# Stick-breaking attention of a three-block network on one Trainium2 core: rounded parts of queries and keys stored by the first product, two heads loaded early, another order on TensorE

## Chip, cores and metric

The kernel runs on one core of one Trainium2 chip, in one launch. The metric is the device time of that core in microseconds (us). The engines are TensorE (PE; its weight loads are listed as PEld), VectorE (DVE), ScalarE (ACT), GpSimd (POOL) and SyncE (SP), which here only issues transfers.

## What is computed

A network of three blocks on 1024 tokens of width 1024. The change lies in the first block, whose first mixer is stick-breaking attention with 8 heads of width 64:

```python
def first_block(x, mem, g_in, w_in, ...):
    h = _rmsnorm(x, g_in[l])
    proj = h @ w_in[l]                              # 1024 x 3584
    q_sb, k_sb, v_sb, u_c, b_c, c_c, q_mem, gate = jnp.split(proj, SPLIT_POINTS, axis=-1)
    y_sb = _stick_breaking_attention(q_sb, k_sb, v_sb)      # 8 heads
    m = _rmsnorm(mem, g_mem[l]); mk, mv = jnp.split(m @ w_mem_kv[l], 2, axis=-1)
    ...

def _stick_breaking_attention(q, k, v):   # per head, query t, key s < t
    # A[t,s] = sigmoid(z_ts) * prod_{s<j<t} (1 - sigmoid(z_tj)),  z = q.k / 8
    return A @ v
```

All of it is float32. Products that need the accuracy are made on TensorE in float32r from two rounded parts: hi is the value rounded to float32r, lo is the rest, value - hi.

## The kernel before, in words

`kernel` builds phases that follow each other. A phase (`Phase`) holds its own tiles and semaphores, and an instruction block with one program for each engine; the next phase begins on every engine when all have ended the last one. Within a phase each engine runs its program in order, and waits are written out by hand with counting semaphores.

The phases around the change, in order: `b1_turn`; `b1_in`, the first product (`late_norm_gemm_phase`); `mem_turn`, `mem_norm` (`norm_phase`) and `mem_kv`, which make the keys and values of the memory attention; `stick` (`stick_phase`); `conv`; `mem`. The products of `b1_in` go to the DRAM tensor `proj1`, transposed, 28 tiles of 128 rows by 1024 tokens. Rows 0 to 511 are the queries, 512 to 1023 the keys, 1024 to 1535 the values. For each tile (pair i, side s) TensorE does 48 products of 128x512 (`half_tile`), VectorE splits the tile's weights (`split`, L66 and L1075) and scales the sums into `out_sb` (`scale_out`, L1081), and ScalarE issues the store (`store`, L969). VectorE's loop is `split(i, s)`, then `scale_out(i - 1, s)`.

`norm_phase` can issue transfers for later phases on SP's queue (its list `ahead`), ahead of the loads of its gain vector (L369). `mem_kv` loads its weights by SP at L116 and splits them on VectorE (L66, L140) before TensorE begins.

`stick_phase` runs over 64 units. A unit j is one head and one block of 128 queries, `units[j] = (head, i)`, with n = i + 1 blocks of 128 keys. Heads go in four pairs, 16 units each, and the two heads of a pair alternate so that n runs 1, 8, 2, 7, 3, 6, 4, 5, 5, 4, 6, 3, 7, 2, 8, 1 in pairs 0 and 2, and 8, 1, 7, 2, ... in pairs 1 and 3. For each unit:

- `score(j)` on TensorE: q times k_hi and k_lo, and a mask, into one or two pieces of up to 512 columns (L1856, L1857, L1859), in a ring of four PSUM banks. `q_two` holds q_hi in its upper 64 partitions and q_lo in its lower 64, and `k_hi` and `k_lo` hold the head twice, so that the contraction over 128 partitions adds both.
- `sigmoids(j)` on ScalarE (L1922): "stay" = sigmoid(-z) of all pieces, then "take" = sigmoid(z), written over a part of `y`. Needs the scan of unit j-3 done.
- on VectorE the scan `later` (a running product of "stay", L1980), then weights = take * later (L1984).
- `turn` on TensorE (L1873): transposes the weights in groups of four blocks, into two PSUM buffers; `copy_turned` on ScalarE copies them to `wT` (L1936), which has three buffers. The values of a pair are turned likewise (L1931).
- `product(j)` on TensorE (L1883): weights times values, two instructions for each block; VectorE copies two results out after every fourth unit (L1958).

ScalarE's loop is `sigmoids(j + 2)`, `copy_turned` of unit j. TensorE's loop is:

```python
for j in range(NU):
    if j + 3 < NU:
        score(j + 3)
    while x < len(turns) and (turns[x][0] == "v" or turns[x][1] <= j):
        turn(x)
        x += 1
    if j >= 2:
        product(j - 2)
```

The rounded parts are made inside this phase. SP loads each head's keys and queries twice into halves of a spare tile (`b_gate` in the trace, L1803, L1805), four transfers of 256 KB. For heads 0 and 1 ScalarE rounds (L1908, L1910) and VectorE subtracts (L1962, L1964) before TensorE can begin. For heads 2 to 7 GpSimd does four instructions a head (L1829, L1831, L1833, L1835) while the units of the pair before run.

Of the kernel before, what the change touches and what calls it, by code (L numbers as in the profile page):

```python
# [8 lines left out]
F32 = mybir.dt.float32  # L9
# [5 lines left out]
P = 128  # L15
# [315 lines left out]
def norm_phase(nc, name, sum_matrix, src, dst, groups, g_vecs, tokens=T, scale_cols=None, shift_cols=None, src_dram=None,  # L331
# [12 lines left out]
    with Phase(nc, name) as ph:  # L344
# [15 lines left out]
        def _(sp):  # L360
# [503 lines left out]
def late_norm_gemm_phase(nc, name, ones, src, w_dram, n_cols, g_vec, out_dram, final_g=None, gate_pair=None, gate_shift=0):  # L864
# [11 lines left out]
    WAYS = 2 if double else 1  # L876
    with Phase(nc, name) as ph:
# [12 lines left out]
        out_sb, sig = ([ph.sb(f"{n}{s}", [P, T]) for s in range(2)] for n in ("out", "sig"))  # L890
        acc = [[ph.ps(f"acc{s}{h}", [P, HALF]) for h in range(NH)] for s in range(2)]
# [11 lines left out]
        gate_sig, gated_ready = [ph.sem(f"gate_sig{s}") for s in range(2)], [ph.sem(f"gated_ready{s}") for s in range(2)]  # L903
        w_view = w_dram.rearrange("(c p) n -> p c n", p=P)
# [32 lines left out]
        def _(act):  # L937
# [32 lines left out]

            def gate_and_store(i, s):
# [6 lines left out]
            for s in range(2):  # L978
                act.sem_inc(copied[s], NH)
                act.sem_inc(out_free[s], 16)  # L980
# [12 lines left out]
            if gate_pair > 0:  # L993
                with act.Fori(0, gate_pair) as i:
                    for s in range(2):
                        store(i, s)
# [6 lines left out]
            for s in range(2):  # L1003
                act.wait_ge(out_free[s], 16 * uses[s] + 16)

# [41 lines left out]
        def _(dve):  # L1047
# [34 lines left out]

            def gate_out(i, s):
# [29 lines left out]
            with dve.Fori(1, gate_pair + 1) as i:  # L1113
# [624 lines left out]
def stick_phase(nc, name, ident, neg_future, qT, kT, vT, y, spare, n_heads):  # L1738
# [11 lines left out]
    V_AT = (5, 9)  # L1750
    units = []
# [19 lines left out]
    with Phase(nc, name) as ph:  # L1771
        q_raw, k_raw = ([spare[:, 4 * n + 2 * b:4 * n + 2 * b + 2, :].rearrange("p a t -> p (a t)") for b in range(2)] for n in range(2))
        take = [y[:, NQ // 2 + b, :] for b in range(SIG)]
        q_two, k_hi, k_lo = ([ph.sb(f"{n}{b}", [P, T], F32R) for b in range(HEADS)] for n in ("q_two", "k_hi", "k_lo"))
        v_raw = [ph.sb(f"v_raw{b}", [P, T]) for b in range(2)]
# [9 lines left out]
        q_loaded, k_loaded, v_loaded = ([ph.sem(f"{n}_loaded{b}") for b in range(2)] for n in ("q", "k", "v"))  # L1785
        hi_ready, split_done, pool_split = ph.sem("hi_ready"), ph.sem("split_done"), ph.sem("pool_split")
# [8 lines left out]
        def _(sp):  # L1795
            def load(hd):
                b = hd % 2
                if hd in (2, 3):
                    sp.wait_ge(split_done, 2 * (hd - 1))
                elif hd >= 4:  # L1800
                    sp.wait_ge(pool_split, 4 * (hd - 3))
                for r in range(2):
                    sp.dma_start(k_raw[b][64 * r:64 * r + 64, :], kT[hd * 64:hd * 64 + 64, :]).then_inc(k_loaded[b], 16)  # L1803
                for r in range(2):
                    sp.dma_start(q_raw[b][64 * r:64 * r + 64, :], qT[hd * 64:hd * 64 + 64, :]).then_inc(q_loaded[b], 16)  # L1805

            def load_v(c):
                if c >= 2:
                    sp.wait_ge(turned_ready, turn_of["v", c - 2, 1] + 1)
# [11 lines left out]

        @block.gpsimd
        def _(pool):
            for hd in range(2, n_heads):
                b, r, done = hd % HEADS, hd % 2, 4 * (hd - 2)
                if hd >= HEADS:
                    pool.wait_ge(piece_ready, pieces_to[PER * (hd // 2 - 1)])
                pool.wait_ge(k_loaded[r], 32 * (hd // 2 + 1))
                nc.gpsimd.tensor_copy(k_hi[b][:, :], k_raw[r][:, :]).then_inc(pool_split, 1)  # L1829
                pool.wait_ge(pool_split, done + 1)  # L1830
                nc.gpsimd.tensor_tensor(k_lo[b][:, :], k_raw[r][:, :], k_hi[b][:, :].bitcast(F32), ALU.subtract).then_inc(pool_split, 1)  # L1831
                pool.wait_ge(q_loaded[r], 32 * (hd // 2 + 1))
                nc.gpsimd.tensor_copy(q_two[b][:, :], q_raw[r][:, :]).then_inc(pool_split, 1)  # L1833
                pool.wait_ge(pool_split, done + 3)
                nc.gpsimd.tensor_tensor(q_two[b][64:P, :], q_raw[r][64:P, :], q_two[b][64:P, :].bitcast(F32),  # L1835
                                        ALU.subtract).then_inc(pool_split, 1)
                pool.wait_ge(pool_split, done + 4)

        @block.tensor
        def _(pe):  # L1840
            def score(j):
                hd, i = units[j]
                b = hd % HEADS
                if j % PER < 2:
                    if hd < 2:
                        pe.wait_ge(split_done, 2 * hd + 2)
                    else:
                        pe.wait_ge(pool_split, 4 * (hd - 1))
# [13 lines left out]
            def turn(x):  # L1862
# [3 lines left out]
                if kind == "v":  # L1866
                    pe.wait_ge(v_loaded[a % 2], 16 * (a // 2 + 1))
# [25 lines left out]
            for j in range(NU):  # L1893
                if j + 3 < NU:
                    score(j + 3)
# [3 lines left out]
                if j >= 2:  # L1899
                    product(j - 2)  # L1900
            product(NU - 2)
# [3 lines left out]
        def _(act):  # L1905
            def split(hd):
                act.wait_ge(k_loaded[hd], 32)
                nc.scalar.activation(k_hi[hd][:, :], k_raw[hd][:, :], ACT.Copy).then_inc(hi_ready, 1)  # L1908
                act.wait_ge(q_loaded[hd], 32)
                nc.scalar.activation(q_two[hd][:, :], q_raw[hd][:, :], ACT.Copy).then_inc(hi_ready, 1)  # L1910

# [26 lines left out]
            split(0)  # L1938
            split(1)
# [13 lines left out]
        def _(dve):  # L1953
# [6 lines left out]
            def split(hd):  # L1960
                dve.wait_ge(hi_ready, 2 * hd + 1)
                nc.vector.tensor_tensor(k_lo[hd][:, :], k_raw[hd][:, :], k_hi[hd][:, :].bitcast(F32), ALU.subtract).then_inc(split_done, 1)  # L1962
                dve.wait_ge(hi_ready, 2 * hd + 2)
                nc.vector.tensor_tensor(q_two[hd][64:P, :], q_raw[hd][64:P, :], q_two[hd][64:P, :].bitcast(F32),  # L1964
                                        ALU.subtract).then_inc(split_done, 1)

# [6 lines left out]
            split(0)  # L1973
            split(1)
# [3477 lines left out]
def first_block(nc, A, C, M, xT):  # L5452
# [4 lines left out]
    mem_kv = scratch("mem_kv", 2 * MEM_W, N_MEM)  # L5457
    all_chunks = [(list(range(KD)), D)]
    first_turn_phase(nc, "b1_turn", ident, A["x"][0], xT)
    late_norm_gemm_phase(nc, "b1_in", ones, xT, A["w_in"][0], W1, A["g_in"][0], p, gate_pair=GATE1 // (2 * P))  # L5460
    with Phase(nc, "b1") as b1:
        y, gate = b1.sb("y", [P, KD, T]), b1.sb("gate", [P, KD, HALF])
        with Phase(nc, "b1m") as m:
# [204 lines left out]
```

## Time and profile before

| | us |
|---|---|
| median of 3 runs | 4560.4 |
| lowest, highest | 4555.65, 4563.99 |
| the profiled execution | 4569.06 |
| its span, first to last instruction | 4567.2 |
| TensorE busy in it | 3881.7 (85%) |
| VectorE busy | 2753.9 (60%) |
| ScalarE busy | 1915.0 (42%) |
| GpSimd busy | 482.3 (11%) |
| `mem_norm`'s first transfer to that of `stick_phase` | 359.56 to 397.18 |
| `stick_phase`, first transfer to last copy out | 397.18 to 604.6 |

The busy shares are means over many phases with different limits; the part that the change touches is the first 605 us. There the views to read are the busy time by stretch, the groups of instructions by line, and the timeline. In a row, "x16" counts instructions, "128x1024 f32<-128x1024 f32" is partitions by elements of output and input, and a time in brackets is how long the engine was idle before, with what released it. "b_y" is the tile into which "take" and the weights are written, "top_squares" holds the constants.

### The profile page before, as it was taken

The page shows a single profiled execution, that of the slowest core. Times are in us where ns is not written, and L with a number is a line of the kernel's source. Part 1 is how long each engine was busy: PE and PEld are TensorE (multiplying, and loading weights), DVE is VectorE, ACT ScalarE, POOL GpSimd, SP SyncE. Part 2 cuts the span into 40 slices and gives each one's busy share as a digit, 9 for nine tenths or more (in the row PEclk, how much of TensorE's full clock was granted, in tenths as well). Part 3 has the DMA queues.
Part 4 walks back from the last instruction along what each step waited for, and adds up shares of the span by engine and source line. Part 5 has one row for each costly group of instructions (what it writes and reads, how often), then busy time and mean ns, then how long its engine had stood idle before and what let it go on. Part 6 is the DMA issues. An engine that isn't in the chain of part 4 may idle for free. (4 is left out here: it accounts for less than half of the span.)

```text
span 4567.2 us, 51409 instructions
## 1 busy us (share of the span) xinstructions
PE 3881.7 (85%) x18727; PEld 3094.5 (68%) x18727; DVE 2753.9 (60%) x3208; ACT 1915.0 (42%) x2588; POOL 482.3 (11%) x347
## 2 busy tenths in 40 slices
PE   8995876899987897889849999999997998756479
PEld 6884744678854773767528888888885786635467
DVE  4235956431115775656469999999996334556852
ACT  2013634211114663224317777777774103454223
POOL 0001313140001212110000101100100400000020
PEclk9997988899998998989969999999997998878789
DMA  3224042122242106146239999999996233534241
GB/s 118 92 87 111 19 142 68 35 87 100 93 160 62 26 14 225 51 149 195 91 141 406 392 386 388 378 386 389 380 383 212 74 97 112 151 103 124 68 147 37
DMA packets 435455, 762.89 MB, mean 167 GB/s; under 512 B 101831, under 2 KB 264199, under 8 KB 434152
## 3 DMA queue, kind: packets, MB, share of 16 engines
q1 hardware_dynamic: 407480, 689.85, 42.9%
q10 hardware_dynamic: 23216, 54.27, 3.1%
q0 software_dynamic: 4608, 16.78, 1.4%
q8 instruction: 91, 1.49, 0.1%
q14 instruction: 60, 0.49, 0.0%
HBM read 643.64 MB, written 114.69 MB: 166 GB/s over the span
## 5 line engine op out<-in xcount | busy, mean ns | idle before, releaser
L71 PE MATMUL b_in_acc<-b_in_acts_hi,b_in_w_hi 128*128 128x512 f32 (+1 forms) x1456 | 573.6, 394 | 48.2 <-POOL b_in_w_lo L1132 20.9
L72 PE MATMUL b_in_acc<-b_in_acts_lo,b_in_w_hi 128*128 128x512 f32 (+1 forms) x1456 | 571.0, 392 | 0.0
L73 PE MATMUL b_in_acc<-b_in_acts_hi,b_in_w_lo 128*128 128x512 f32 (+1 forms) x1456 | 570.7, 392 | 0.0
L3965 DVE TENSOR_TENSOR experts_w_lo<-top_xT,experts_w_hi 128x2048 fp32r<-128x2048 f32 x192 | 437.3, 2290 | 62.4 <-ACT experts_w_hi L3910 62.4
L66 DVE CAST b_in_w_hi<-b_in_w 128x1024 fp32r<-128x1024 f32 (+1 forms) x91 | 65.2, 716 | 652.9 <-PE b_in_acc L73 641.6
L3965 DVE TENSOR_TENSOR experts_w_lo<-experts_ring,experts_w_hi 128x2048 fp32r<-128x2048 f32 x192 | 435.8, 2288 | 31.5 <-ACT experts_w_hi L3910 29.4
L3910 ACT ACTIVATE experts_w_hi<-top_xT 128x2048 fp32r<-128x2048 f32 x192 | 367.6, 1919 | 127.2 <-PE experts_gate L73 74.1
L3910 ACT ACTIVATE experts_w_hi<-experts_ring 128x2048 fp32r<-128x2048 f32 x192 | 367.8, 1921 | 114.7 <-PE experts_up L73 64.7
L71 PEld LDWEIGHTS b_in_acc<-b_in_acts_hi,b_in_w_hi 128*128 128x128 f32 (+1 forms) x1456 | 275.4, 189 | 111.7 <-POOL b_in_w_lo L1132 21.5
L72 PEld LDWEIGHTS b_in_acc<-b_in_acts_lo,b_in_w_hi 128*128 128x128 f32 (+1 forms) x1456 | 275.5, 189 | 58.7 <-issue 0.5
L73 PEld LDWEIGHTS b_in_acc<-b_in_acts_hi,b_in_w_lo 128*128 128x128 f32 (+1 forms) x1456 | 275.1, 189 | 58.8
L71 PE MATMUL experts_gate<-experts_w_hi,experts_xg_hi 128*128 128x512 f32 x512 | 201.8, 394 | 4.8 <-DVE experts_w_lo L3965 4.8
L71 PE MATMUL experts_y_ps<-experts_w_hi,experts_act_hi 128*128 128x512 f32 x512 | 205.3, 401 | 0.0
L71 PE MATMUL experts_up<-experts_w_hi,experts_xg_hi 128*128 128x512 f32 x512 | 200.8, 392 | 2.6 <-DVE experts_w_lo L3965 2.6
L73 PE MATMUL experts_y_ps<-experts_w_hi,experts_act_lo 128*128 128x512 f32 x512 | 200.3, 391 | 0.0
L73 PE MATMUL experts_gate<-experts_w_hi,experts_xg_lo 128*128 128x512 f32 x512 | 200.3, 391 | 0.0
L72 PE MATMUL experts_gate<-experts_w_lo,experts_xg_hi 128*128 128x512 f32 x512 | 200.0, 391 | 0.0
L72 PE MATMUL experts_y_ps<-experts_w_lo,experts_act_hi 128*128 128x512 f32 x512 | 199.6, 390 | 0.0
L73 PE MATMUL experts_up<-experts_w_hi,experts_xg_lo 128*128 128x512 f32 x512 | 199.4, 389 | 0.0
L72 PE MATMUL experts_up<-experts_w_lo,experts_xg_hi 128*128 128x512 f32 x512 | 199.4, 389 | 0.0
L760 ACT ACTIVATE b_in_out<-b_in_acc 128x512 f32<-128x512 f32 x76 | 45.5, 599 | 358.5 <-PE b_in_acc L73 357.8
L974 ACT ACT_TABLE_LOAD x8 | 10.3, 1283 | 375.6 <-DVE b_in_out L1081 366.0
(737 smaller groups left out, 8707.6 us busy)
## 6 DMA issues: line engine op xcount, KB each, us to landing
experts_ring<-in_w_gate SPq DMA_DIRECT2D x128, 1024.0 KB, 7.0
top_xT<-in_w_up SPq DMA_DIRECT2D x128, 1024.0 KB, 9.9
experts_ring<-in_w_down SPq DMA_DIRECT2D x64, 1024.0 KB, 9.3
top_xT<-in_w_down SPq DMA_DIRECT2D x64, 1024.0 KB, 9.2
b_in_w<-in_w_in SPq DMA_DIRECT2D x90, 512.0 KB, 3.9
proj<-b_in_out ACTq DMA_DIRECT2D x90, 512.0 KB, 2.7
b_gate<-proj SPq DMA_DIRECT2D x48, 256.0 KB, 5.0
x_spill<-top_xT SPq DMA_DIRECT2D x3, 4096.0 KB, 14.0
```

The source lines that it names most:

```text
L66: return nc.vector.tensor_copy(hi, x)
L71: nc.tensor.matmul(out, w_hi, x_hi, start=start, stop=False)
L72: nc.tensor.matmul(out, w_hi, x_lo, start=False, stop=False)
L73: return nc.tensor.matmul(out, w_lo, x_hi, start=False, stop=stop)
L760: nc.scalar.activation(out_sb[s][0:m, at(h)], acc[s][h][0:m, :], ACT.Copy).then_inc(copied[s], 1)
L974: nc.scalar.activation(sig[s][:, at(h)], out_sb[s][:, at(h)], ACT.Sigmoid).then_inc(gate_sig[s], 1)
L3910: nc.scalar.activation(w_hi[n % HIS][:, :, :], ring[n % RING], ACT.Copy).then_inc(hi_ready, 1)
L3965: nc.vector.tensor_tensor(w_lo[n % HIS][:, :, :], ring[n % RING], w_hi[n % HIS][:, :, :].bitcast(F32), ALU.subtract).then_inc(lo_ready, 1)
```

## The change

In the first product, `round_and_store` (ScalarE) and `part_out` (VectorE) take the place of `store` and `scale_out` for the first 8 tiles, the queries and keys. They make hi and lo of the scaled tile and store both, in two DRAM tensors `qk1_hi` and `qk1_lo`; those rows of `proj1` are no longer written. `stick_phase` loads the parts straight into `q_two`, `k_hi` and `k_lo`, six transfers of 256 KB for a head, and has no splitting left: the GpSimd program is gone, as are `split(0)` and `split(1)` on ScalarE and VectorE. The tiles of heads 0 and 1 and of the first two chunks of values are allocated around the memory phases, and `mem_norm` issues their 14 loads, now behind those of its gain. TensorE's loop has another order and does the product one unit earlier and the scores after it.

```diff
@@ norm_phase, SP
-            for tile, rows, ahead_loaded in ahead:
-                sp.dma_start(tile, rows).then_inc(ahead_loaded, 16)
             if g_vecs:
...
+            for tile, rows, ahead_loaded in ahead:
+                sp.dma_start(tile, rows).then_inc(ahead_loaded, 16)
@@ late_norm_gemm_phase
+            def round_and_store(i, s):
+                act.wait_ge(part_free[s], i * 32 + 32)
+                for h in range(NH):
+                    act.wait_ge(copied[s], i * NH + (NH + h + 1))
+                    nc.scalar.activation(parts[0][s][:, at(h)], out_sb[s][:, at(h)], ACT.Copy).then_inc(part_hi_ready[s], 1)
+                act.wait_ge(part_hi_ready[s], i * NH + NH)
+                act.dma_start(parts_dram[0][ds(col0(i, s, P, False), P), :], parts[0][s][:, :].bitcast(F32)).then_inc(part_free[s], 16)
+                act.wait_ge(part_lo_ready[s], i * NH + NH)
+                act.dma_start(parts_dram[1][ds(col0(i, s, P, False), P), :], parts[1][s][:, :].bitcast(F32)).then_inc(part_free[s], 16)
...
+            def part_out(i, s):
+                scale_out(i, s)
+                dve.wait_ge(part_free[s], i * 32 + 32)
+                for h in range(NH):
+                    dve.wait_ge(part_hi_ready[s], i * NH + (h + 1))
+                    tt(parts[1][s][:, at(h)], out_sb[s][:, at(h)], parts[0][s][:, at(h)].bitcast(F32),
+                       ALU.subtract).then_inc(part_lo_ready[s], 1)
...
-            with dve.Fori(1, gate_pair + 1) as i:
+            if part_pairs:
+                with dve.Fori(1, part_pairs + 1) as i:
+                    for s in range(2):
+                        split(i, s)
+                        part_out(i - 1, s)
+            with dve.Fori(part_pairs + 1, gate_pair + 1) as i:
@@ stick_phase, SP
             def load(hd):
-                b = hd % 2
-                if hd in (2, 3):
-                    sp.wait_ge(split_done, 2 * (hd - 1))
-                elif hd >= 4:
-                    sp.wait_ge(pool_split, 4 * (hd - 3))
+                b = hd % HEADS
+                if hd >= HEADS:
+                    sp.wait_ge(piece_ready, pieces_to[PER * (hd // 2 - 1)])
                 for r in range(2):
-                    sp.dma_start(k_raw[b][64 * r:64 * r + 64, :], kT[hd * 64:hd * 64 + 64, :]).then_inc(k_loaded[b], 16)
-                for r in range(2):
-                    sp.dma_start(q_raw[b][64 * r:64 * r + 64, :], qT[hd * 64:hd * 64 + 64, :]).then_inc(q_loaded[b], 16)
+                    for dst, part in ((k_hi, k_parts[0]), (k_lo, k_parts[1]), (q_two, q_parts[r])):
+                        sp.dma_start(dst[b][64 * r:64 * r + 64, :].bitcast(F32), part[hd * 64:hd * 64 + 64, :]).then_inc(loaded[b], 16)
...
-            load(0)
-            load(1)
-            load_v(0)
-            load_v(1)
@@ stick_phase, GpSimd
-        @block.gpsimd
-        def _(pool):
-            for hd in range(2, n_heads):
...
@@ stick_phase, TensorE
             for j in range(NU):
-                if j + 3 < NU:
-                    score(j + 3)
                 while x < len(turns) and (turns[x][0] == "v" or turns[x][1] <= j):
                     turn(x)
                     x += 1
-                if j >= 2:
-                    product(j - 2)
-            product(NU - 2)
+                if j >= 1:
+                    product(j - 1)
+                if j + 3 < NU:
+                    score(j + 3)
             product(NU - 1)
@@ stick_phase, ScalarE and VectorE
-            split(0)
-            split(1)
@@ first_block
-    late_norm_gemm_phase(nc, "b1_in", ..., gate_pair=GATE1 // (2 * P))
+    late_norm_gemm_phase(nc, "b1_in", ..., gate_pair=GATE1 // (2 * P), parts_dram=qk_parts)
...
+            first = [b1s.sb(f"{n}{b}", [P, T], dt)[:, :] for n, dt in (("q_two", F32R), ("k_hi", F32R), ("k_lo", F32R), ("v_raw", F32)) for b in range(2)]
...
+                norm_phase(nc, "mem_norm", ones, memT, memT, all_chunks, pieces(A["g_mem"][0]), tokens=N_MEM,
+                           ahead=[(dst, rows, first_loaded) for dst, rows in first_heads(first, q_parts, k_parts, v_rows)])
```

`first_heads` lists, for heads 0 and 1 and each half, the loads of `q_two`, `k_hi` and `k_lo`, and then the two loads of values.

## Rows read from the trace of the kernel before

**Rows 1.** Busy time by stretch: stretch, length, engines with counts, PEclk, DMA, GB/s.

```profile
414.40:452.00 37.60, 25.06 (x162) 22.88 (x161) 34.26 (x24) 20.69 (x51) 17.88 (x8) 0.77 0.40 99
490.00:528.00 38.00, 27.41 (x205) 25.75 (x203) 36.47 (x31) 22.50 (x55) 19.35 (x8) 0.94 0.00 1
561.50:598.90 37.40, 32.97 (x266) 31.14 (x265) 35.40 (x39) 26.99 (x69) 0.00 (x0) 1.00 0.00 1
```

**Rows 2.** Groups by line, VectorE, 414.3 to 598.9: busy us, mean ns, idle before.

```profile
L1980 DVE TENSOR_TENSOR_SCAN stick_later<-stick_stay,stick_ones 128x128 f32<-128x128 f32 (+7 forms) x64 | 100.3, 1567 | 4.8 <-ACT stick_stay L1922 4.3
L1984 DVE TENSOR_TENSOR b_y<-b_y,stick_later 128x128 f32<-128x128 f32 (+7 forms) x64 | 65.5, 1024 | 6.7
L1958 DVE COPY b_y<-stick_o 64x256 f32<-64x256 f32 x28 | 11.8, 422 | 2.6 <-PE stick_o L1883 1.8
```

**Rows 3.** The same view, 561.5 to 598.9, pair 3, without GpSimd work.

```profile
L1980 DVE TENSOR_TENSOR_SCAN stick_later<-stick_stay,stick_ones 128x1024 f32<-128x1024 f32 (+7 forms) x16 | 21.6, 1353 | 0.1
L1984 DVE TENSOR_TENSOR b_y<-b_y,stick_later 128x1024 f32<-128x1024 f32 (+7 forms) x16 | 12.1, 759 | 1.7
```

**Rows 4.** Timeline (start, length, engine): a multiplication with and without GpSimd beside it.

```profile
511.62 4.40 POOL L1835 TENSOR_TENSOR stick_q_two<-b_gate,stick_q_two 64x1024 fp32r<-64x1024 f32 x1
...
513.99 3.12 DVE L1984 TENSOR_TENSOR b_y<-b_y,stick_later 128x1024 f32<-128x1024 f32 x1
...
564.00 1.23 DVE L1984 TENSOR_TENSOR b_y<-b_y,stick_later 128x1024 f32<-128x1024 f32 x1
```

**Rows 5.** Timeline of TensorE and ScalarE around units of eight blocks.

```profile
557.47 0.48 PE L1856 MATMUL stick_piece<-stick_k_hi,stick_q_two 128*128 128x512 f32 x1
...
558.53 0.39 PE L1873 MATMUL stick_turned<-top_squares,b_y 128*128 128x128 f32 x2
...
559.24 1.08 ACT L1922 ACTIVATE stick_stay<-stick_piece 128x512 f32<-128x512 f32 x2
...
560.19 1.11 ACT L1922 ACTIVATE b_y<-stick_piece 128x512 f32<-128x512 f32 x2
...
561.14 1.14 ACT L1936 ACTIVATE stick_wT<-stick_turned 128x512 f32<-128x512 f32 x2
...
566.27 1.95 PE L1883 MATMUL stick_o<-stick_wT,stick_v 128*128 128x128 f32 x16
```

**Rows 6.** Timeline, the start of the stick phase.

```profile
397.18 1.19 SPq L1803 DMA_DIRECT2D b_gate<-proj  x2
...
397.37 0.22 DVE L1968 CAST stick_mask<-top_squares 128x128 fp32r<-128x128 f32 x1
...
410.21 1.94 PE L1873 MATMUL stick_turned<-top_squares,stick_v_raw 128*128 128x128 f32 x8 [15.88 <-DMA stick_v_raw<-proj]
...
414.40 0.90 DVE L1980 TENSOR_TENSOR_SCAN stick_later<-stick_stay,stick_ones 128x128 f32<-128x128 f32 x1 [3.22 <-ACT stick_stay L1922]
```

**Rows 7.** Busy time by stretch, while keys and queries arrive, then values.

```profile
401.00:407.00 6.00, 0.00 (x0) 0.00 (x0) 2.45 (x2) 2.39 (x3) 0.00 (x0) 0.50 1.03 238
409.00:411.00 2.00, 0.79 (x4) 0.82 (x5) 1.07 (x2) 0.93 (x1) 0.00 (x0) 0.50 1.07 391
```

**Rows 8.** Timeline of the memory phases: gain loads, weight loads, first use.

```profile
359.56 3.65 SPq L369 DMA_DIRECT2D mem_norm_gain<-in_g_mem  x8
...
372.58 12.93 SPq L116 DMA_DIRECT2D mem_kv_w<-in_w_mem_kv  x4
376.14 0.69 DVE L66 CAST mem_kv_w_hi<-mem_kv_w 128x1024 fp32r<-128x1024 f32 x1 [3.82 <-DMA mem_kv_w<-in_w_mem_kv]
```

**Rows 9.** Timeline, the last turn and the last products of the stick phase.

```profile
599.02 1.06 PE L1873 MATMUL stick_turned<-top_squares,b_y 128*128 128x128 f32 x8 [1.41 <-DVE b_y L1984]
...
599.92 3.74 PE L1883 MATMUL stick_o<-stick_wT,stick_v 128*128 128x128 f32 x32
```

**Rows 10.** Busy time by stretch, two tiles of the first product.

```profile
67.00:90.00 23.00, 23.00 (x103) 19.06 (x102) 6.24 (x8) 0.00 (x0) 0.00 (x0) 1.00 0.34 111
```

More of the change, by code:

```diff
@@ L876, in late_norm_gemm_phase @@
     WAYS = 2 if double else 1
+    part_pairs = parts_dram[0].shape[0] // (2 * P) if parts_dram else 0
     with Phase(nc, name) as ph:
@@ L890, in late_norm_gemm_phase @@
         out_sb, sig = ([ph.sb(f"{n}{s}", [P, T]) for s in range(2)] for n in ("out", "sig"))
+        parts = [[ph.sb(f"part_{n}{s}", [P, T], F32R) for s in range(2)] for n in ("hi", "lo")] if part_pairs else None
         acc = [[ph.ps(f"acc{s}{h}", [P, HALF]) for h in range(NH)] for s in range(2)]
@@ L903, in late_norm_gemm_phase @@
         gate_sig, gated_ready = [ph.sem(f"gate_sig{s}") for s in range(2)], [ph.sem(f"gated_ready{s}") for s in range(2)]
+        part_hi_ready, part_lo_ready = [ph.sem(f"part_hi_ready{s}") for s in range(2)], [ph.sem(f"part_lo_ready{s}") for s in range(2)]
+        part_free = [ph.sem(f"part_free{s}") for s in range(2)]
         w_view = w_dram.rearrange("(c p) n -> p c n", p=P)
@@ L992, in _ @@
             inverse(1)
-            if gate_pair > 0:
-                with act.Fori(0, gate_pair) as i:
+            if part_pairs:
+                with act.Fori(0, part_pairs) as i:
+                    for s in range(2):
+                        round_and_store(i, s)
+            if gate_pair > part_pairs:
+                with act.Fori(part_pairs, gate_pair) as i:
                     for s in range(2):
@@ L1004, in _ @@
                 act.wait_ge(out_free[s], 16 * uses[s] + 16)
+                if part_pairs:
+                    act.wait_ge(part_free[s], 32 * part_pairs + 32)
         @block.tensor
@@ L1112, in _ @@
             dve.wait_ge(inv_ready, 2)
-            with dve.Fori(1, gate_pair + 1) as i:
+            if part_pairs:
+                with dve.Fori(1, part_pairs + 1) as i:
+                    for s in range(2):
+                        split(i, s)
+                        part_out(i - 1, s)
+            with dve.Fori(part_pairs + 1, gate_pair + 1) as i:
                 for s in range(2):
@@ L1735, in _, with first_heads, stick_phase @@
                         split(j, g)
-def stick_phase(nc, name, ident, neg_future, qT, kT, vT, y, spare, n_heads):
+def first_heads(tiles, q_parts, k_parts, vT):
+    out = []
+    for hd in range(2):
+        rows = slice(64 * hd, 64 * hd + 64)
+        for r in range(2):
+            half = slice(64 * r, 64 * r + 64)
+            out += [(tiles[2 * n + hd][half, :].bitcast(F32), part[rows, :]) for n, part in enumerate((q_parts[r], k_parts[0], k_parts[1]))]
+    return out + [(tiles[6 + c], vT[c * P:(c + 1) * P, :]) for c in range(2)]
+def stick_phase(nc, name, ident, neg_future, q_parts, k_parts, vT, y, first, first_loaded, n_heads):
     NQ = T // P
@@ L1771, in stick_phase @@
     with Phase(nc, name) as ph:
-        q_raw, k_raw = ([spare[:, 4 * n + 2 * b:4 * n + 2 * b + 2, :].rearrange("p a t -> p (a t)") for b in range(2)] for n in range(2))
         take = [y[:, NQ // 2 + b, :] for b in range(SIG)]
-        q_two, k_hi, k_lo = ([ph.sb(f"{n}{b}", [P, T], F32R) for b in range(HEADS)] for n in ("q_two", "k_hi", "k_lo"))
-        v_raw = [ph.sb(f"v_raw{b}", [P, T]) for b in range(2)]
+        q_two, k_hi, k_lo = (first[2 * m:2 * m + 2] + [ph.sb(f"{n}{b}", [P, T], F32R)[:, :] for b in range(2, HEADS)]
+                             for m, n in enumerate(("q_two", "k_hi", "k_lo")))
+        v_raw = first[6:8]
         v_sb = [ph.sb(f"v{b}", [P, NQ, P]) for b in range(2)]
@@ L1784, in stick_phase @@
         o_ps = [ph.ps(f"o{b}", [P, 2, 2 * P]) for b in range(2)]
-        q_loaded, k_loaded, v_loaded = ([ph.sem(f"{n}_loaded{b}") for b in range(2)] for n in ("q", "k", "v"))
-        hi_ready, split_done, pool_split = ph.sem("hi_ready"), ph.sem("split_done"), ph.sem("pool_split")
+        loaded, v_loaded = [ph.sem(f"loaded{b}") for b in range(HEADS)], [ph.sem(f"v_loaded{b}") for b in range(2)]
         consts_ready, piece_ready = ph.sem("consts_ready"), ph.sem("piece_ready")
@@ L1866, in turn @@
                 if kind == "v":
-                    pe.wait_ge(v_loaded[a % 2], 16 * (a // 2 + 1))
+                    if a < 2:
+                        pe.wait_ge(first_loaded, FIRST_LOADS)
+                    else:
+                        pe.wait_ge(v_loaded[a % 2], 16 * (a // 2))
                     src, blocks = v_raw[a % 2], range(4 * g, 4 * g + 4)
```

59 lines of the change are left out of this document (19 added, 40 removed).

## Prediction

> **What bounds the kernel now.** I read the views in this order: busy time by stretch, the groups of instructions by line, the timeline, and the timeline of the memory stages ahead of `stick_phase`. VectorE sets the pace of `stick_phase`: in the stretches of [rows 1] it is busy 34.26 of 37.60, 36.47 of 38.00 and 35.40 of 37.40 us. From its first scan at 414.40 us to the end of its last product of weights at 598.9 us, 184.5 us, it has 100.3 + 65.5 + 11.8 = 177.6 us of listed work [rows 2], and of its idle time only 1.1 us waits for ScalarE (a second wait of 3.2 us lies ahead of the first scan) and 1.8 us for TensorE. But the same 16 units cost it different times. Pair 3 (561.5 to 598.9 us), where GpSimd is idle, takes 21.6 us of scans and 12.1 us of multiplications [rows 3]. Four such pairs would be 86.4 + 48.4 = 134.8 us; the trace has 165.8 us. The missing 31.0 us are instructions drawn out while GpSimd splits queries and keys: a 128x1024 multiplication begun inside a GpSimd subtraction takes 3.12 us, and alone it takes 1.23 us [rows 4]. The stretch 490 to 528 us has a DMA share of 0.00 and yet holds such slow instructions [rows 1, 4], so the cause isn't the loads.
>
> The Trainium skill says the same in "SBUF — State Buffer", section "Who interferes with whom": VectorE instructions with two SBUF inputs contend with GpSimd instructions that read SBUF, and DMA doesn't contend with them. By that rule all of the excess goes with the GpSimd work; [rows 4] agree (1.23 against 3.12 us).
>
> **b1_in.** The first product is bound by TensorE: 23.00 of 23.00 us between 67 and 90 us, while VectorE works 6.24 us [rows 10]. For 8 of the 28 tiles the change adds two ScalarE copies and two VectorE subtractions of 128x512, by the nearest rows 0.69 us or less each, some 1.4 us per engine and tile, plus the wait of VectorE for the two copies, 1.5 us with the hand-over. Behind that wait stands `split` of the next tile. VectorE's 6.24 us in 23 us, two tiles, leave it 8 us of idle time a tile [rows 10], more than these 3 us. ScalarE only stores there. One more store of 512 KB per tile in 10.9 us meets a DMA share of 0.34. I take nothing; if that cover were gone it would be 3 us x 8 = 24 us.
>
> **GpSimd's work removed.** Removing the 24 GpSimd instructions takes back the excess (31.0 us) if VectorE remains the bound. TensorE then also comes earlier to the products for which VectorE waited (1.8 us), and the 1.1 us for ScalarE I also take as gone. The clean length is 184.5 - 33.9 = 150.6 us. Heads 2 to 7 now come by six DMAs of 256 KB each instead of four, 3.1 MB per pair of heads. At 238 GB/s [rows 7] that is 13.2 us within a pair of 37 us, and no engine waits behind them: hidden.
>
> **The new order.** Before, TensorE did `score(j+3)`, `turn(j)`, `product(j-2)`; now it does `turn(j)`, `product(j-1)`, `score(j+3)`. Its work is the same: in 561.5 to 598.9 us it was busy 32.97 of 37.40 us already [rows 1]. What is new is a closed loop: product of a large unit, scores of the large unit two later, ScalarE's sigmoids of these scores, ScalarE's copy of the turned weights (which is behind these sigmoids in its program), and then the next large product, which now waits for that copy at once. From [rows 5], for eight blocks: a product is 16 instructions in 1.95 us, and 32 take 3.74 us [rows 9], so 0.112 each and 1.79 us; the scores 557.47 to 558.53, 1.06 us; the hand-over 0.25 us; the second piece's "stay" 0.48 us; from 560.19 to 561.14 for the "take", 0.95 us; the copy 1.14 us. Sum 5.7 us. Scaling each part by blocks gives 5.1 for seven, 4.6 for six, 4.0 for five. VectorE's 37.4 us for pair 3 [rows 1] hold 16 units and three of its four double copies out (0.84 us each by the mean of 422 ns in [rows 2]), so it needs 38.2 us a pair and 4.78 us for two units. Where two pairs of heads meet, the sizes 7, 8, 8, 7 follow: 21.6 us of loop against 19.1 us. TensorE falls 2.5 us behind, of which the lead of the scores (from the end of unit j to the scan of j+3 VectorE has the work of two units, 4.6 us without a copy out; the path is one block's turn 0.1, a product of eight 1.8, scores of seven 0.9 and hand-overs and sigmoid 1.1, together 3.9 us, and shorter elsewhere) takes up 0.9 us. So 1.6 us at each of three borders, 4.8 us; between them the loop is shorter than 4.78 and catches up. To this I add 1.5 us for the first units, where TensorE starts from the low level of its clock, 1.2 GHz (granted 0.50 in [rows 7]) and the second scan waits for its sigmoids. Loss 6.3 us; bounds: nothing, since the old order has no such wait in pair 3, and the 21.6 us of rival B. The steady part becomes 150.6 + 6.3 = 156.9 us, 27.6 us less.
>
> **The start.** Before, the first load is issued at 397.18, TensorE's first transpose waits until 410.21, and the first scan begins at 414.40, 4.19 us later [rows 6]. With heads 0 and 1 already in SBUF, TensorE waits only for the two constant casts, which end 397.6. That alone would be 12.6 us. But the 14 early loads are put on SP's queue in front of the weights of `mem_kv`. SP has issued its eight gain loads by 363.2 us [rows 8]; 14 issues of 0.6 us (1.19 for two, [rows 6]) last until 371.8, just ahead of the 372.58 at which the next phase's loads start now, so the issue is covered by about 0.7 us. The bytes are not covered: twelve loads of 262 kB at 238 GB/s are 13.2 us, and two of 524 kB at 391 GB/s 2.7 us [rows 7]. From 365.1 (issue plus 1.9 us: the 3.56 us from issue to use of a weight in [rows 8], less some 1.7 for its bytes) they last until 381.0. The first weight, issued at 372.58 and used at 376.14 [rows 8], then lands about 382.8: 6.7 us later, and the whole of `mem_kv` with it, since each of its later steps follows from the first. Net gain at the start 12.6 - 6.7 = 5.9 us. Bounds: 12.6, if the weight's packets don't wait, and 0, if the loads go at half the rate over the last half.
>
> The Trainium skill, "DMA: Bandwidth & Descriptors", section "Queues, rings and completion order", says that SP owns one row of rings whose descriptors are consumed in ring order. By that rule the weights wait for the early loads, as in my sum; with interleaving it would be the other bound. No row here shows two SP transfers overtaking each other.
>
> **The tail.** After the last `turn`, 32 product instructions run in 3.74 us, units 61, 62 and 63 [rows 9]. `product(61)` is now done earlier, 14 instructions less, 1.6 us; but the last product must wait for ScalarE's copy, so I take 0.9 us.
>
> **The sum.** 27.6 + 5.9 + 0.9 = 34.4 us off. The profiled execution took 4569.1 us (span 4567.2) and would take 4534.7 us; against the median of the runs, 4560.4 us, 4526 us.
>
> **The rivals.** A: the order costs nothing and the weights don't wait for the early loads: 33.9 + 12.6 + 0.9 = 47.4 us off, 4513 us. For it speaks that VectorE never waited in pair 3; against it the loop's 5.7 us. Chance 0.12. B: the loop holds everywhere, not only at the borders, if each hand-over is 0.6 us longer than I read. Then eight loops of a pair last 43.6 us instead of VectorE's 38.2, so 21.6 us are lost instead of 6.3: 19.1 us off, 4541 us. For it speaks that the worked average of a loop is 4.85 us against 4.78, no reserve at all. Chance 0.16. C: the edit does not relieve VectorE, because the long instructions come from something else: only the start and tail remain, less the loss, 0.5 us off, 4560 us. The pairs in [rows 4] are against it. Chance 0.03. D, slower: TensorE's clock. TensorE needs some 36.2 us per pair at the full level of 2.4 GHz (72 blocks x 0.224 for products, 80 x 0.113 for turns [rows 9], 16 scores of together 11 us: 72 blocks at the 1.06 for eight are 9.5, and small ones have a fixed part on top). At the low level, 1.2 GHz, this would be 72.4 us, 290 us for the stage, 105 us more than now: with start and tail 4659 us. It decides once the mean granted clock of the stage falls under 36.2 x 4 / 191 = 0.76. The stage now has 0.77 in its first fifth, where TensorE idles most, and 0.94 and 1.00 later [rows 1], and the denser order gives TensorE fewer idle times. With a cover of `b1_in` that fails, the slower side gets 0.05.
>
> **How the numbers follow.** Forecast 0.64, A 0.12, B 0.16, C 0.03, D 0.05. The forecast's own range, with a start of 2 to 9 us and a loss of 2 to 11 us, is 4518 to 4535. To hold 8 in 10 it is drawn out over most of A and B: 4513 to 4542. A measurement of this kernel tells about 0.2% (9 us) from no change. A, B and the forecast are faster by more: 0.92; I give 0.90, since B could end lower than its price. Within 0.2%: C and the edge of B, 0.05. Slower: 0.05.
>
> **What the profile after would show.** No GpSimd instruction between 400 and 600 us, and every 128x1024 multiplication near 1.23 us: the main step. First weight cast of `mem_kv` near 383 us and first scan near 408.5 us: the start. From first scan to the end of the last multiplication 157 us, with VectorE's waits for ScalarE's "stay" of 1 to 2 us near units 15 to 19, 31 to 35 and 47 to 51: the loop. If these waits are in every group of four units, B is right; if none, A. A granted clock under 0.8 in the stage would be D. `b1_in` must keep its 10.9 us per tile.

## The result and the profile after

| | before | after |
|---|---|---|
| median of the runs, us | 4564.9 (7 runs) | 4544.4 (7 runs) |
| time of the profiled execution, its span, us | 4569.1, 4567.2 | 4544.4, 4542.6 |
| first weight cast of `mem_kv`, us from the span's start | 376.1 | 383.8 |
| first scan of `stick_phase` | 414.4 | 408.5 |
| first scan to the end of the last multiplication | 184.5 | 163.3 |
| from there to the last copy out | 5.7 | 4.9 |
| all that follows | 3963 | 3966 |

The ratio of the times is 0.9956 (0.9944 to 0.9967): 20.5 us or 0.4% faster. The forecast was 34.4 us, and its time, 4526 us, and the upper end of its range, 4542 us, both lie below the median of 4544.4 us. The forecast's time was counted from before's median of three runs, 4560.4 us; its median of seven is 4564.9 us, 4.5 us more. A second comparison of the same two kernels gave 4539.7 against 4565.0 us, 25.2 us off, ratio 0.9941 (0.9929 to 0.9953).

Busy time by stretch, kernel after: the whole stage first, then three stretches that answer to [rows 1] (the first 37.6 us, 490 to 528 us, and the 16 units of pair 3). Columns as there: stretch, length, PE, PEld, DVE, ACT and POOL with counts, granted clock, DMA share, GB/s.

```profile
408.51:571.84 163.33, 145.69 (x1109) 133.56 (x1108) 144.37 (x156) 116.94 (x291) 0.00 (x0) 0.97 0.28 62
...
408.50:446.10 37.60, 32.51 (x237) 30.00 (x237) 32.97 (x33) 28.29 (x70) 0.00 (x0) 0.89 0.37 82
490.00:528.00 38.00, 34.70 (x271) 31.95 (x270) 34.23 (x38) 27.86 (x67) 0.00 (x0) 1.00 0.35 75
532.30:571.80 39.50, 35.71 (x274) 32.35 (x272) 35.54 (x38) 27.89 (x72) 0.00 (x0) 1.00 0.00 1
```

The same view of before, for the whole stage:

```profile
414.40:598.88 184.48, 147.34 (x1098) 138.79 (x1096) 173.70 (x156) 118.44 (x291) 56.90 (x24) 0.92 0.14 35
```

VectorE does the same 156 instructions in 144.4 instead of 173.7 us, 29.3 us less, and GpSimd does nothing. But the stage became only 21.2 us shorter: VectorE's idle time in it rose from 10.8 to 19.0 us. And pair 3, which had no GpSimd work beside it before either, now takes 39.5 us where it took 37.4 us [rows 1]. These are the 8.2 us that the rest of this text is about.

The groups of VectorE in the stage after (busy us, mean ns of one, then idle time before them and what ended it), as [rows 2]:

```profile
L1987 DVE TENSOR_TENSOR_SCAN stick_later<-stick_stay,stick_ones 128x128 f32<-128x128 f32 (+7 forms) x64 | 86.7, 1354 | 13.5 <-ACT stick_stay L1940 12.8
L1991 DVE TENSOR_TENSOR b_y<-b_y,stick_later 128x128 f32<-128x128 f32 (+7 forms) x64 | 48.5, 759 | 7.1 <-DVE stick_later L1987 0.5
```

Scans and multiplications now have in all four pairs the means they had in pair 3 before, 1354 and 759 ns against 1353 and 759 [rows 3]; together 135.2 us. The new number is behind the bar: 12.8 us of waiting for ScalarE's "stay", 2.4 of it ahead of the first scan. In the stage of before it was 1.1 us.

### The profile page after: what moved, and what is told of

It is laid out like the page before. It is cut to its first block and busy times, and to the rows that moved or that the text cites. A ratio compares the mean times of both kernels' runs of the same rounds, so it can differ in the third digit from the quotient of the medians.

```text
span 4542.6 us, 51470 instructions
## 1 busy us (share of the span) xinstructions
PE 3877.7 (85%) x18727; PEld 3091.1 (68%) x18727; DVE 2736.7 (60%) x3220; ACT 1919.1 (42%) x2600; POOL 429.0 (9%) x323
## 5 line engine op out<-in xcount | busy, mean ns | idle before, releaser
L71 PEld LDWEIGHTS b_in_acc<-b_in_acts_hi,b_in_w_hi 128*128 128x128 f32 (+1 forms) x1456 | 275.0, 189 | 113.1 <-POOL b_in_w_lo L1168 21.2
```

The costliest lines, as they stand in the source:

```text
L71: nc.tensor.matmul(out, w_hi, x_hi, start=start, stop=False)
```

## The experiments

Each kernel has the edit shown and nothing else; the diffs are shortened, and "..." marks what is left out. "Stage" is the time from the first scan to the end of the last multiplication, in the profiled execution.

| kernel | median us | ratio to before | stage us | first scan |
|---|---|---|---|---|
| before | 4564.4, 4565.0 | | 184.5 | 414.4 |
| changed kernel, again | 4539.7 | 0.9941 (0.9929 to 0.9953) | 163.2 | 408.5 |
| old order | 4527.2 | 0.9924 (0.9910 to 0.9938) | 151.7 | 409.2 |
| order alone | 4564.5 | 1.0000 (0.9991 to 1.0009) | 188.5 | 412.4 |
| late scores only | 4530.1 | 0.9930 (0.9917 to 0.9944) | 154.3 | 408.3 |
| early product only | 4531.7 | 0.9929 (0.9916 to 0.9943) | 152.0 | 409.6 |
| GpSimd work put back | 4553.3 (one time) | | 177.7 | 410.0 |
| no early loads | 4550.4 | 0.9966 (0.9954 to 0.9978) | 163.5 | 421.0 |
| split early loads | 4525.0 | 0.9895 (0.9878 to 0.9911) | 151.7 | 402.0 |

The ratio is that to before in the same comparison: before's median is 4564.4 us for the four kernels on TensorE's order and 4565.0 us for the other four.

**The old order in the changed kernel.** The edit in TensorE's loop:

```diff
 for j in range(NU):
+    if j + 3 < NU:
+        score(j + 3)
     ...
-    if j >= 1:
-        product(j - 1)
-    if j + 3 < NU:
-        score(j + 3)
+    if j >= 2:
+        product(j - 2)
+product(NU - 2)
 product(NU - 1)
```

> The changed kernel with TensorE's old order (scores, turns, product two units back) in the stick phase, all else kept. The changed kernel took 163.3 us from its first scan to the end of the last multiplication, with 12.8 us of VectorE waiting for the stay sigmoids, where 150.6 us is the length without waits. Theory L (the new order closes a loop product, scores, sigmoids, copy, product): 151 us, VectorE waits under 1.5 us, first scan again near 408.5 us, and some 12 us less in all than the changed kernel (about 32 us less than before). Rival N (the waits come from something else in the change, such as the slower start or the loads of six parts): the waits stay near 12 us, and the total stays near that of the changed kernel.

It came to 4527.2 us, 37.1 us under before where the changed kernel in its second comparison is 25.2 us under it, and the stage to 151.7 us, 11.6 us less than 163.3. The medians differ by 11.9 us, but they come from two comparisons and the intervals of the two ratios overlap a little (0.9910 to 0.9938 and 0.9929 to 0.9953); the 11.6 us of the traces carry the reading. Its stage by stretch, and its waits in it (engine and line, waited for, us in total, times, longest):

```profile
409.23:560.94 151.71, 139.00 (x1098) 130.99 (x1096) 142.97 (x156) 117.42 (x291) 0.00 (x0) 0.98 0.30 65
```

```profile
ACT stick_wT L1955 <- PE stick_turned L1898: 31.1, 42, 1.9
...
PE stick_turned L1898 <- DVE b_y L1992: 9.2, 12, 2.5
DVE stick_later L1988 <- ACT stick_stay L1941: 3.5, 2, 3.3
```

And the waits of the changed kernel in its stage:

```profile
ACT stick_stay L1940 <- PE stick_piece L1879: 35.4, 26, 2.2
...
PE stick_turned L1898 <- ACT stick_wT L1954: 13.5, 23, 1.4
DVE stick_later L1987 <- ACT stick_stay L1940: 12.8, 19, 2.4
...
PE stick_turned L1898 <- DVE b_y L1991: 3.0, 2, 2.3
```

With the old order everybody waits for VectorE: TensorE 9.2 us for the weights, ScalarE 31.1 us for their turned form, and VectorE itself for nobody after its first two scans (3.3 of the 3.5 us lie ahead of the first, the rest ahead of the second). With the new order ScalarE waits for scores (35.4 us), TensorE for ScalarE's copies (13.5 us) and VectorE for ScalarE (12.8 us): a ring. VectorE is idle 8.7 us with the old order and 19.0 with the new, 10.2 us by the unrounded values; the remaining 1.4 us of the 11.6 is its busy time, 142.97 against 144.37 us, with the same means for each instruction. In the timeline of the old order 48 scans start some 0.08 us before the end of the multiplication ahead of them, in that of the changed kernel only 31: a scan that has waited has lost this overlap.

**The order alone, in the kernel before.** The same edit the other way round, on before.

> The kernel before with only the new order on TensorE. GpSimd's splitting still draws VectorE out, which gives the loop time. Theory L: in the stretches without GpSimd work VectorE waits as in the changed kernel (3 to 5 us in pairs 2 and 3), in those with it hardly; the stage from first scan to last multiplication goes from 184.5 to 186 to 190 us, the tail is 0.8 us shorter, total 1 to 5 us slower. Rival N: no new waits, total 0 to 1 us faster by the tail.

Ratio 1.0000, stage 188.5 us, 4.0 us longer; the scan's wait is

```profile
DVE stick_later L1979 <- ACT stick_stay L1921: 9.7, 13, 3.1
```

so even with a VectorE that needs 30 us more, the ring shows. It costs less there (4.0 against 11.6 us), and the timeline shows why. GpSimd works from 412.0 to 430.7, from 458.2 to 478.7 and from 507.0 to 527.3 us. Of the 12 scans that wait for ScalarE after the first, 11 lie outside these stretches and the twelfth, at 507.59, had waited since before the third began; the border between pairs 0 and 1, where VectorE waits 2.5 us in the changed kernel, costs 0.4 us here. Where GpSimd draws VectorE's work out, the ring's time is covered. The 4.0 us are a reading of the traces: the medians, expected 1 to 5 us apart, don't show them. What the order gives back is the tail, 5.7 to 4.9 us.

**Which half of the order.** Late scores only: `turn`, `product(j - 2)`, `score(j + 3)`. Early product only: `score(j + 3)`, `turn`, `product(j - 1)`.

> The changed kernel, order turn(j), product(j-2), score(j+3): the scores come late as in the change, the product keeps its old distance of two units. Theory L needs both: with the product two units back its copy is long done, the loop is open, so 151 to 153 us for the stage and some 11 us less than the changed kernel. Rival S (late scores alone do it, since ScalarE gets them after the product): 160 to 164 us, as in the changed kernel.

> The changed kernel, order score(j+3), turn(j), product(j-1): scores early as before, product one unit back. Theory L: the product may wait for its copy, but the scores of the next units are already in PSUM, so ScalarE is not held up: 151 to 154 us for the stage. Rival P (the early product alone does it, TensorE stands at the copy): 158 to 164 us.

In both, VectorE's wait for ScalarE stays near the 3.5 us of the old order (first line late scores, second line early product):

```profile
DVE stick_later L1988 <- ACT stick_stay L1941: 4.0, 5, 2.4
```

```profile
DVE stick_later L1987 <- ACT stick_stay L1940: 3.8, 3, 3.3
```

Stages of 154.3 and 152.0 us against 151.7 with neither and 163.3 with both. Late scores cost 2.6 us, the early product 0.3, and the two together 11.6. It takes both halves. My reading of the code: with `product(j - 2)` the product finds its copy already made, so TensorE seldom stands ahead of the scores (the late scores' trace has 5 waits of TensorE for ScalarE, 3.8 us, where the changed kernel has 23 of 13.5 us at the turns and 5 of 0.8 us at the products); with `score(j + 3)` first the product may wait, and the scores are out already. The two theories that one half alone carries the loss fall.

**The changed kernel again.**

> The changed kernel once more, on the chip and in the rounds of the others here. In its first trace the stick phase ends 27.8 us earlier than before, while the medians differed by 20.5 us. If what is left is the variation of the long unchanged part behind it, the medians now differ by 24 to 30 us; if the change costs 5 us or more somewhere later, they stay at 18 to 22 us.

4539.7 us, 25.2 us off, and the stage 163.2 us. So the 20.5 us of the first comparison is at the low end. "All that follows" the stage is 3953 to 3966 us over the ten profiled executions of this text, before among them. The changed kernel's two executions have 3962 and 3966 us there and before has 3963, so the traces show no cost of the change after the stage, but one of a few us would not stand out. The 27.9 us that the traces show up to there stand against medians 25.2 and 20.5 us apart, and no run here takes the 2.7 and 7.4 us between apart.

**GpSimd's work put back.** On the kernel with the old order: 24 GpSimd instructions of the removed kinds (copy, subtraction, copy, subtraction of 64 partitions, for each of heads 2 to 7), on a spare tile whose values nobody reads, and a memset of that tile ahead of them. No part of the computation is left out.

```diff
+nc.gpsimd.memset(a, 1.0)
+for hd in range(2, n_heads):
+    pool.wait_ge(piece_ready, ...)
+    nc.gpsimd.tensor_copy(b, a)
+    nc.gpsimd.tensor_tensor(b, a, a, ALU.subtract)
+    nc.gpsimd.tensor_copy(b, a)
+    nc.gpsimd.tensor_tensor(b[64:P, :], a[64:P, :], a[64:P, :], ALU.subtract)
```

> Old order on TensorE, parts from the first product, and 24 GpSimd instructions of the sizes of the removed ones (copies and subtractions on the spare tile, whose results nobody reads), in the same stretches, with no semaphore to any other engine. Theory G (GpSimd reading SBUF draws VectorE's two-input instructions out): the stage from first scan to last multiplication goes from 151.7 back up to 178 to 185 us, with multiplications of 128x1024 taking 3.1 us again. Rival W (it was the waits on the split parts and SP's loads): 152 us.

The stage went from 151.7 to 177.7 us, with no transfer and no wait added for VectorE. Groups of VectorE, then those of GpSimd:

```profile
L2009 DVE TENSOR_TENSOR_SCAN stick_later<-stick_stay,stick_ones 128x128 f32<-128x128 f32 (+7 forms) x64 | 98.6, 1541 | 5.3 <-ACT stick_stay L1962 4.9
L2013 DVE TENSOR_TENSOR b_y<-b_y,stick_later 128x128 f32<-128x128 f32 (+7 forms) x64 | 60.1, 940 | 7.1 <-ACT b_y L1962 0.5
```

```profile
L1878 POOL TENSOR_TENSOR b_gate<-b_gate 64x1024 f32<-64x1024 f32 x6 | 19.6, 3275 | 0.5
L1874 POOL COPY b_gate<-b_gate 128x1024 f32<-128x1024 f32 x11 | 19.5, 1776 | 54.5 <-PE stick_piece L1902 54.0
L1876 POOL TENSOR_TENSOR b_gate<-b_gate 128x1024 f32<-128x1024 f32 x6 | 12.6, 2094 | 0.5
```

51.7 us of GpSimd in these three lines lengthen scans by 12.0 and multiplications by 11.5 us, 23.5 of the 26.0 us (one of the 24 instructions lies ahead of the first scan). So GpSimd's work beside VectorE's is the cause of most of the excess in before, and it is not tied to the data: these instructions touch a tile that no other engine uses in the stage. It gave back 26.0 of the 32.8 us between 151.7 and before's 184.5 us, a stage just under the 178 to 185 us expected. The instructions are not the removed ones to the letter: they write f32 and not float32r, and GpSimd is busy 51.7 us with them where it was busy 56.9 us. What makes up the other 6.8 us stays open. The multiplications of 128x1024 did not all take the 3.1 us expected either: the five that ran beside GpSimd took 1.81 to 2.67 us, the three others 1.23 us. The Trainium skill's rule in "SBUF — State Buffer", "Who interferes with whom", that VectorE and GpSimd share one pair of ports, agrees with these 26.0 us.

**No early loads.** The changed kernel with the 14 transfers for heads 0 and 1 issued as the first thing of `stick_phase` instead of in `mem_norm`.

```diff
-norm_phase(nc, "mem_norm", ..., ahead=[... first_heads(...)])
+norm_phase(nc, "mem_norm", ...)
 ...
@@ stick_phase, SP
+for dst, rows in first_loads:
+    sp.dma_start(dst, rows).then_inc(first_loaded, 16)
 for p in range(1, PAIRS):
```

> The changed kernel with the 14 loads issued at the start of the stick phase and none early. Theory Q (early loads hold up the weights of mem_kv in SP's queue): mem_kv's first weight is cast near 376.1 again, not at 383.8, the stick phase begins 7.5 us earlier, its 4.2 MB take 16 us from 399, and the first scan comes at 419 us, 10.5 us later than the changed kernel's 408.5; in all 8 to 12 us slower than the changed kernel. Rival: the weight is late for another reason and stays near 383 us; then first scan 426 us.

4550.4 us, 10.6 us slower than the changed kernel in the same comparison; first scan at 421.0 us and first weight cast back at 375.2 us (376.1 in before). In the changed kernel the cast is at 383.8 us.

```profile
375.15 0.69 DVE L66 CAST mem_kv_w_hi<-mem_kv_w 128x1024 fp32r<-128x1024 f32 x1 [3.79 <-DMA mem_kv_w<-in_w_mem_kv]
```

```profile
383.81 0.69 DVE L66 CAST mem_kv_w_hi<-mem_kv_w 128x1024 fp32r<-128x1024 f32 x1 [12.74 <-DMA mem_kv_w<-in_w_mem_kv]
```

VectorE waits 12.74 us for the weight instead of 3.79. The early loads are therefore worth 12.5 us at the first scan, after paying 8.7 us of delay in `mem_kv`.

**Split early loads, old order.** The old order, and seven of the 14 transfers issued in `mem_turn`, whose SP queue has nothing behind its two row loads, the other seven in `mem_norm`.

```diff
@@ transpose_phase, SP, behind the loads of its rows
+for tile, part, ahead_loaded in ahead:
+    sp.dma_start(tile, part).then_inc(ahead_loaded, 16)
@@ first_block
+early = [(dst, rows, first_loaded) for dst, rows in first_heads(...)]
-transpose_phase(nc, "mem_turn", ident, A["mem"][0], memT, N_MEM)
+transpose_phase(nc, "mem_turn", ident, A["mem"][0], memT, N_MEM, ahead=early[:7])
 norm_phase(nc, "mem_norm", ...
-           ahead=[... first_heads(...)])
+           ahead=early[7:])
```

> Old order, and the 14 early loads split: 7 issued in mem_turn behind its rows, 7 in mem_norm behind its gain. Theory Q: 1.8 MB are through by 363 us and the rest by 373.5 us, so the first weight is cast near 377 us instead of 383.3, the first scan comes at 402.5 us instead of 409.2, the stage stays 151.7 us, and the kernel is 6 us faster than with the old order alone, some 42 us faster than before. Rival: the bytes only move the wait to the gain or the rows, and the first scan comes at 407 us or later.

Timeline: two of the early loads, the weight cast and the first scan.

```profile
352.38 0.57 SPq L266 DMA_DIRECT2D b1s_q_two<-qk_hi  x1
...
363.50 0.47 SPq L375 DMA_DIRECT2D b1s_k_hi<-qk_hi  x1
...
376.30 0.69 DVE L66 CAST mem_kv_w_hi<-mem_kv_w 128x1024 fp32r<-128x1024 f32 x1 [3.75 <-DMA mem_kv_w<-in_w_mem_kv]
```

```profile
402.01 0.42 DVE L1990 TENSOR_TENSOR_SCAN stick_later<-stick_stay,stick_ones 128x128 f32<-128x128 f32 x1 [3.26 <-ACT stick_stay L1943]
```

The weight is not delayed, the first scan is at 402.0 us, 12.4 us earlier than before and 7.2 us earlier than with the old order alone, the stage is 151.7 us, and the median is 4525.0 us: 40 us or 1.05% under before, and 14.8 us under the changed kernel. By its ratio this is the fastest of all kernels here, though the interval (0.9878 to 0.9911) just touches that of the old order alone; the traces show the 7.2 us between the two.

## Why the prediction was right or wrong

**What bounds the kernel: right.** Scans and multiplications were to fall from 165.8 to 134.8 us; they are 135.2 us. A 128x1024 multiplication takes 1.23 us everywhere, and the experiment that put GpSimd back returned 26.0 us.

**The clean length: nearly right.** Forecast 150.6 us; the kernel without the new order has 151.7 us.

**The new order: here the prediction failed, in the size of its loss.** It was forecast at 6.3 us and is 11.6 us. The ring itself was read rightly. The third border between pairs, after (timeline; the bracket is the idle time before and what ended it):

```profile
530.99 0.29 DVE L1991 TENSOR_TENSOR b_y<-b_y,stick_later 128x128 f32<-128x128 f32 x1
...
533.14 1.12 ACT L1954 ACTIVATE stick_wT<-stick_turned 128x512 f32<-128x512 f32 x2
...
533.83 0.33 PE L1898 MATMUL stick_turned<-top_squares,b_y 128*128 128x128 f32 x1 [0.59 <-ACT stick_wT L1954]
...
534.31 2.05 PE L1908 MATMUL stick_o<-stick_wT,stick_v 128*128 128x128 f32 x16 [0.16 <-ACT stick_wT L1954]
...
536.95 0.98 ACT L1940 ACTIVATE stick_stay<-stick_piece 128x512 f32<-128x512 f32 x2 [2.18 <-PE stick_piece L1879]
...
537.82 0.99 ACT L1940 ACTIVATE b_y<-stick_piece 128x512 f32<-128x512 f32 x2
...
537.96 2.02 DVE L1987 TENSOR_TENSOR_SCAN stick_later<-stick_stay,stick_ones 128x896 f32<-128x896 f32 x1 [1.27 <-ACT stick_stay L1940]
...
538.66 1.12 ACT L1954 ACTIVATE stick_wT<-stick_turned 128x512 f32<-128x512 f32 x2
...
539.84 2.05 PE L1908 MATMUL stick_o<-stick_wT,stick_v 128*128 128x128 f32 x16 [0.16 <-ACT stick_wT L1954]
```

Product of eight blocks at 534.31, the seven-block scores behind it (their sigmoids start at 536.95), "take" at 537.82, the copy at 538.66, and the next large product at 539.84: one round in 5.53 us, forecast 5.1 to 5.7. Over the sizes 7, 8, 8, 7 the large products begin at 523.72, 528.80, 534.31, 539.84 and 545.04 us, 21.3 us for the four rounds; forecast 21.6. VectorE needs 19.1 us for these units. The difference is 2.2 us, and VectorE waits 2.35 us there (0.40, 1.27, 0.16 and 0.52 ahead of four scans). So all of it reaches VectorE: from the scan of unit 44 to that of unit 52 it takes 21.2 us here and 19.1 us with the old order. The failed step is the sentence that the lead of the scores takes up 0.9 us: the trace shows no part of it taken up, and each border costs the full difference.

That sentence rests on a path that the trace shows to be longer. From the end of a unit to the scan three units on it counted one `turn`, a product, scores, hand-overs and a sigmoid, 3.9 us, against two units of VectorE's work, 4.6 us (which is 0.7 us, not 0.9, in its own numbers). At this border unit 47 ends at 531.28 us (the first row, 530.99 + 0.29) and the scan of unit 50 starts at 537.96, 6.7 us later. The path took for granted that TensorE reaches the `turn` of unit 47 at once. It reaches it at 533.83, 2.55 us late: before it stand the `turn` of the eight blocks of unit 46, a product, scores, and the wait of 0.59 us for ScalarE's copy. VectorE was occupied for 5.4 us of this time, a double copy out included, and waited 1.27 us. At the first border the figures for unit 15 are the same: 2.5 us late, and 6.7 us to the scan of unit 18. The waits at the other borders are of the same size: 2.5 and 2.8 us at the first two, 7.7 us for all three where I had 4.8; and 1.5 us in the middle of pairs 0 and 2, where two units of five blocks follow each other, for which I had nothing. The first units cost 1.2 us of waits for ScalarE, near the 1.5 us forecast (0.3 of them the old order has too). The three sums of waits for ScalarE, 7.7 + 1.5 + 1.2, are the 12.8 us of the trace less the 2.4 ahead of the first scan; 1.4 us of lost overlap were in no term.

I had also closed the ring in one place only, the product that waits for its copy. The row at 533.83 shows a second one just ahead of it: the small `turn` of the next unit waits 0.59 us for the first of the two turned buffers, so TensorE stands there first, 23 times and 13.5 us in the stage, and at the products only 5 times and 0.8 us. I did not run a kernel with a third buffer, so what that wait alone is worth stays open.

**Rival A** (the order costs nothing) is refuted by the old order's 11.6 us; **rival B** (a ring at every unit, 21.6 us) by the places of the waits: 18 scans of the 63 after the first, all at borders, middles and the start. The truth lies between forecast and B. **C** is refuted by the means of the multiplications. **D** did not come: the mean granted clock in the stage is 0.97, against 0.92 in the stage before. (Its 0.113 us for a turned block is not what [rows 9] give, 1.06 us for eight or 0.13 each; the threshold would be 0.79 and not 0.76, which changes nothing.)

**The start: right in its mechanism; that it fits to 0.1 us is luck, since errors of 1 us cancel.** First scan 5.9 us earlier, as forecast. The first weight came 7.7 us later (forecast 6.7), the stick phase then began 7.4 us later, and the end of the mask cast to the first scan took 3.5 us where 4.2 was taken. SP issued the early loads from 362.84 to 371.5 us, ahead of the next phase, as forecast (14 issues of 0.6 us from 363.2 end at 371.6 and not at 371.8, a slip that changes nothing); their bytes held the weights back, and the kernel with split loads shows that this was avoidable. The bound of 12.6 us that I had given for "no delay" is what that kernel got, 12.4 us.

**b1_in: right.** Two stretches of 23 us, as [rows 10], in the tiles with rounded parts:

```profile
67.00:90.00 23.00, 23.00 (x103) 19.06 (x102) 9.68 (x14) 2.40 (x4) 0.00 (x0) 1.00 0.49 171
72.00:95.00 23.00, 23.00 (x103) 19.06 (x102) 8.82 (x12) 2.40 (x4) 0.00 (x0) 1.00 0.38 137
```

TensorE remains full with the same 103 matmuls; VectorE has 9.68 us instead of 6.24.

**The tail: right.** 5.7 to 4.9 us, 0.8 where 0.9 was forecast.

**The sum.** In traces, 184.5 to 163.3 in the stage, 5.9 at the start and 0.8 at the end are 27.9 us, where 34.4 was forecast; the 6.5 us between are the order's 5.3 and the clean length's 1.1, up to rounding. The median moved 25.2 and 20.5 us in the two comparisons. So of the 18.4 us between the forecast's 4526 and the measured 4544.4 us, 6.5 are these terms, 4.5 the other median of before, and 7.4 the difference between trace and median that no run takes apart. The loss alone would have left the time inside the range of 4513 to 4542 us; with the other two it lies 2.4 us above.

## What to carry to other kernels

When a change relieves the engine that sets the pace, cost every other edit against the faster pace: this order cost 4 us while GpSimd held VectorE back and 11.6 us once it no longer did, and two halves that each cost 0.3 and 2.6 us closed a ring together. Where the sum of a ring exceeds what the pacing engine needs, count the full difference at each place; credit a lead only if a row shows its wait being absorbed, and start its path where the engine really is in its program, not where the data is ready. Put early loads on a queue at a point where nothing urgent is behind their bytes: covering the issues is not enough.

## What the runs showed of the hardware

GpSimd drew out VectorE's instructions over a tile that no other engine touches: in the kernel with its work put back, the mean of the 128x1024 multiplication is 1751 ns, and 1225 ns in the changed kernel.

```profile
L2013 DVE TENSOR_TENSOR b_y<-b_y,stick_later 128x1024 f32<-128x1024 f32 x8 | 14.0, 1751 | 1.3 <-ACT b_y L1962 0.5
```

```profile
L1991 DVE TENSOR_TENSOR b_y<-b_y,stick_later 128x1024 f32<-128x1024 f32 x8 | 9.8, 1225 | 1.3 <-DVE stick_later L1987 0.5
```

With the 14 early loads issued just ahead, an issue itself became slow. In the changed kernel SP's first weight load of `mem_kv` took 0.38 us to issue and the second 4.52 us (the row's second number); without early loads the two together took 1.00 us.

```profile
372.35 4.52 SPq L116 DMA_DIRECT2D mem_kv_w<-in_w_mem_kv  x1
```

```profile
371.62 1.00 SPq L116 DMA_DIRECT2D mem_kv_w<-in_w_mem_kv  x2
```

The longest issue of these weights is 4.19 us in the changed kernel's second trace and 3.63 us with the old order, and 0.58 us with the split loads, without early loads, and in before. I had costed the queue as issues and bytes; that an issue behind these loads can last seven times as long was not in the sum. Here SP had nothing else to do.
